# Gathering the experts' token rows as ready-made high and low parts

## The reference

```python
comb = jnp.einsum("tk,tke->te", w, jax.nn.one_hot(eid, N_EXPERTS, dtype=jnp.float32))
y = jnp.zeros((B * S, D), jnp.float32)
for e in range(N_EXPERTS):
    hid = jax.nn.silu(t @ w1[e]) * (t @ w3[e])
    y = y + comb[:, e:e + 1] * (hid @ w2[e]).astype(jnp.float32)
```

## Time and profile before

| | |
|---|---|
| median of 3 runs | 2202.26 us (2196.2 to 2210.37) |
| profiled execution, its time | 2203.71 us |
| its span in the trace | 2201.9 us |
| busy over the span | PE 96%, PEld 84%, DVE 75%, ACT 50%, POOL 21% |
| mean granted TensorE clock | 0.978 |

### The profile page before, as it was taken

The page is one execution under the profiler, slowest core; times in us unless marked ns, Lnnn a source line. Parts: engine busy times, 40 slices in busy tenths (PEclk is TensorE's granted clock), DMA queues, the critical chain, the costliest instruction groups (busy, mean ns, idle before and its releaser), DMA issues. The chain is left out here.

```text
span 2201.9 us, 34859 instructions
## 1 busy us (share of the span) xinstructions
PE 2115.3 (96%) x13433; PEld 1839.4 (84%) x13433; DVE 1655.9 (75%) x2247; ACT 1111.8 (50%) x1291; POOL 455.8 (21%) x239
## 2 busy tenths in 40 slices
PE   6999999999999999999999998999979999999996
PEld 6998999559998998999658997999957777777775
DVE  5665887548666765778538655788789999999998
ACT  4343353334433433354324343524348888888885
POOL 8600180809004500081718100000010000000000
PEclk9999999999998999999999999999989999999999
DMA  8854564436655655464336653435649999999994
GB/s 260 267 183 141 158 213 141 143 125 226 211 176 186 232 184 178 145 200 154 134 134 211 199 193 96 153 116 166 235 155 362 369 369 378 364 362 377 367 366 171
DMA packets 238996, 484.33 MB, mean 220 GB/s; under 512 B 10612, under 2 KB 178848, under 8 KB 222528
## 3 DMA queue, kind: packets, MB, share of 16 engines
q1 hardware_dynamic: 226880, 443.58, 57.5%
q0 software_dynamic: 11424, 37.44, 5.1%
q10 hardware_dynamic: 608, 2.14, 0.2%
HBM read 482.03 MB, written 1.09 MB: 219 GB/s over the span
## 5 line engine op out<-in xcount | busy, mean ns | idle before, releaser
L748 PE MATMUL misc<-xh,ring_low 128*128 128x256 f32 x1536 | 427.9, 279 | 0.0
L747 PE MATMUL misc<-xl,high_b 128*128 128x256 f32 x1408 | 394.0, 280 | 9.4 <-DVE xl L2117 6.9
L749 PE MATMUL misc<-xh,high_b 128*128 128x256 f32 x1408 | 392.0, 278 | 0.0
L748 PEld LDWEIGHTS misc<-xh,ring_low 128*128 128x128 f32 x1536 | 291.9, 190 | 3.4
L2779 DVE TENSOR_TENSOR ring_low<-ring,high_b 128x2048 fp32r<-128x2048 f32 x128 | 287.1, 2284 | 0.0
L747 PEld LDWEIGHTS misc<-xl,high_b 128*128 128x128 f32 x1408 | 267.2, 190 | 13.7 <-DVE xl L2117 7.1
L749 PEld LDWEIGHTS misc<-xh,high_b 128*128 128x128 f32 x1408 | 267.0, 190 | 0.0
L2126 DVE TENSOR_TENSOR ring_low<-ring,high_b 128x2048 fp32r<-128x2048 f32 x88 | 226.2, 2611 | 39.7 <-ACT high_b L1613 39.7
L1890 ACT ACTIVATE high_b<-ring 128x2048 fp32r<-128x2048 f32 x124 | 235.7, 1914 | 33.9 <-DMA ring<-in_w_dram 33.0
L1644 ACT ACTIVATE arena<-arena 128x256 f32<-128x256 f32 x88 | 36.8, 418 | 427.7 <-DVE arena L2160 427.7
L1310 PE MATMUL misc<-high_b,ue 128*128 128x512 f32 x512 | 204.2, 399 | 1.9 <-DVE ue L2822 1.2
(11 more groups left out here) (426 smaller groups left out, 4964.1 us busy)
## 6 DMA issues: line engine op xcount, KB each, us to landing
ring<-in_w_dram SPq DMA_DIRECT2D x128, 1024.0 KB, 7.8
ring<-in_w_in_dram SPq DMA_DIRECT2D x72, 1024.0 KB, 5.5
ring_d<-in_w_dram SPq DMA_DIRECT2D x128, 512.0 KB, 5.2
ring<-in_ffn_w_gate_dram SPq DMA_DIRECT2D x44, 1024.0 KB, 5.4
ring<-in_ffn_w_up_dram SPq DMA_DIRECT2D x44, 1024.0 KB, 7.8
ring_d<-in_ffn_w_down_dram SPq DMA_DIRECT2D x88, 512.0 KB, 7.3
arena<-in_w_ada_dram POOLq DMA_DIRECT2D x48, 512.0 KB, 4.4
ring<-in_w_out_dram SPq DMA_DIRECT2D x20, 1024.0 KB, 4.9
```

Source lines behind the costliest of these rows:

```text
L747: pe.matmul(dst, wh, ml, start=start, stop=False, **kw)
L748: pe.matmul(dst, wl, mh, start=False, stop=False, **kw)
L749: return pe.matmul(dst, wh, mh, start=False, stop=stop, **kw)
```

## The change

The token rows are split once, ahead of all pairs: ScalarE copies u2 into uh (two instructions of 128x1024, put between the high copies of the first weights), VectorE writes u2 minus uh into ul (two of 128x1024). gather no longer reads u2 in fp32; it runs two passes, one over uh and one over ul, with fp32r matmuls against sel, which is now fp32r as well. The result of a block lies in the bank as block, expert, part, slot, in the order of ue, so that a group fills a whole bank, and ScalarE copies all 512 columns to ue in one instruction. VectorE's tokens (L2822) is gone, and ScalarE's copy sets the bank free. In ScalarE's list tokens 0 and 1 and gate3 now stand ahead of the high copy of the next pair's block 0, and tokens 2 and 3 behind it. u2, sel, both and join move to other addresses; the branch experts, which does not run here, gets two waits.

```diff
--- before.py
+++ after.py
@@ -209,6 +209,9 @@
         hidh, hidl = over("hidh", [2, SEQ]), over("hidl", [2, SEQ])
         beside(A_X)
         xh, xl = over("xh", [KD, SEQ]), over("xl", [KD, SEQ])
+        beside(A_X + 2 * KD * SEQ + NT * D)
+        sel = over("sel", [NT, 2 * CAP])
+        A_JOIN = low_at[0]
         beside(ARENA)
         x = sb("x", [P, NT, D])
         x_rows = x[:, :, :]
@@ -354,12 +357,14 @@
         comb, place = route(EP), route(EP)
         logit = route(N_GROUPS + EXPERTS)
         number = route(1)
-        at[0] = A_X
-        u2 = part([NT, D])
-        sel = part([NT, 2 * CAP])
+        at[0] = A_JOIN
+        join = part([CAP])
+        assert at[0] <= A_OSQ
+        u2 = y2
+        uh, ul = (a[:, :, :].rearrange("p a b -> p (a b)").rearrange("p (t d) -> p t d", t=NT) for a in (xh, xl))
+        at[0] = A_HID + 4 * SEQ
         both = part([2, 2 * BLK])
-        join = part([CAP])
-        assert at[0] <= A_X + 2 * KD * SEQ
+        assert at[0] <= A_X
         at[0] = A_OUT
         out_e = part([D])
         selw = part([NT, 2 * CAP])
@@ -461,6 +466,9 @@
         rows_in = sem("rows_in")
         gained = sem("gained")
         zeroed = sem("zeroed")
+        u2_rows = sem("u2_rows")
+        uh_ready = sem("uh_ready")
+        ul_ready = sem("ul_ready")
         rt_in = sem("rt_in")
         rt_exp = sem("rt_exp")
         y_final = sem("y_final")
@@ -478,7 +486,6 @@
         xs_high = sem("xs_high")
         xs_low = sem("xs_low")
         xh_ready = sem("xh_ready")
-        ue_high = sem("ue_high")
         y_ready = sem("y_ready")
         scattered = sem("scattered")
         lo_ready = sem("lo_ready")
@@ -1290,14 +1297,22 @@
 
                 def gather(i, groups, before=0):
 
-                    for q in groups:
-                        b = claim3(i, TOKENS[q] - before)
-                        for kk in range(2):
-                            k = 2 * q + kk
-                            for t in range(NT):
-                                mm = pe.matmul(b[:, kk * P:(kk + 1) * P], u2[:, t, k * P:(k + 1) * P], sel[:, t, :],
-                                               start=(t == 0), stop=(t == NT - 1))
-                        mm.then_inc(filled, 1)
+                    banks = {}
+                    for part_, rows_ in enumerate((uh, ul)):
+                        if before and part_ and groups[0] == 0:
+                            pe.wait_ge(ul_ready, NT)
+                        for q in groups:
+                            if not part_:
+                                banks[q] = claim3(i, TOKENS[q] - before)
+                            b = banks[q].rearrange("p (k h s c) -> p k s h c", k=2, h=2, s=2)
+                            for kk in range(2):
+                                k = 2 * q + kk
+                                for t in range(NT):
+                                    mm = pe.matmul(b[:, kk, part_], rows_[:, t, k * P:(k + 1) * P],
+                                                   sel[:, t, :].rearrange("p (h c) -> p h c", h=2),
+                                                   start=(t == 0), stop=(t == NT - 1))
+                            if part_:
+                                mm.then_inc(filled, 1)
 
                 def gate_up_e(i, half, j):
 
@@ -1355,7 +1370,9 @@
 
                 g0 = 2 * DEPTH * NF
                 pe.wait_ge(sel_ready, 1)
-                gather(0, range(4), 16)
+                pe.wait_ge(uh_ready, NT)
+                gather(0, range(0, 2), 16)
+                gather(0, range(2, 4), 16)
                 pe.wait_ge(zero_ready, 1)
                 with pe.Fori(0, EXPERTS // 2) as i:
                     for j in TOKENS:
@@ -1924,9 +1941,8 @@
 
                     for q in groups:
                         wait_pair_filled(act, i, F_TOKENS[q] if turn_ == 0 else q - 3)
-                        act.activation(ue[:, 2 * q:2 * q + 2, :, 0:CAP],
-                                       bank_of(M0 + TOKENS[q])[:, 0:2 * P].rearrange("p (a b c) -> p a b c", a=2, b=2),
-                                       ACT.Copy).then_inc(ue_high, 1)
+                        act.activation(ue[:, 2 * q:2 * q + 2, :, :].rearrange("p a b c -> p (a b c)"),
+                                       bank_of(M0 + TOKENS[q]), ACT.Copy).then_inc(drained[(M0 + TOKENS[q]) % 4], 1)
 
                 def first_weights(i, part_):
 
@@ -1953,11 +1969,11 @@
                     for c in range(CPE):
                         high_d(i, 1, c)
                     products(i, 1, 7)
+                    tokens(i, (0, 1))
+                    gate3(i, 1)
                     if not last:
                         high(i + 1, 0, 0)
-                    tokens(i, range(2))
-                    gate3(i, 1)
-                    tokens(i, range(2, 4))
+                    tokens(i, (2, 3))
                     if not last:
                         for x in range(1, 3):
                             high(i + 1, 0, x)
@@ -2033,6 +2049,10 @@
             act.activation(stat[:, 58:60], konst[:, K_CNT:K_CNT + 2], ACT.Exp)
             wait_slot_read(act, RING["wout2"] + 3)
             for x_ in range(4):
+                if x_ == 2:
+                    for t in range(NT):
+                        act.wait_ge(u2_rows, t + 1)
+                        act.activation(uh[:, t, :], u2[:, t, :], ACT.Copy).then_inc(uh_ready, 1)
                 n = RING["moe"] + x_
                 act.wait_ge(loaded[n % SLOTS], LOAD * (n // SLOTS + 1))
                 act.activation(high_b[:, n % SLOTS, :], ring[:, n % SLOTS, :], ACT.Copy).then_inc(high_in[n % SLOTS], 1)
@@ -2738,8 +2758,8 @@
 
             def token_rows(t):
                 dve.wait_ge(gained, t + 1)
-                link(dve.scalar_tensor_tensor(out=token(t), in0=token(t), scalar=rstd[:, t:t + 1],
-                                              in1=by_part(shrow), op0=ALU.mult, op1=ALU.add))
+                dve.scalar_tensor_tensor(out=token(t), in0=token(t), scalar=rstd[:, t:t + 1],
+                                         in1=by_part(shrow), op0=ALU.mult, op1=ALU.add).then_inc(u2_rows, 1)
 
             def placing():
 
@@ -2765,13 +2785,13 @@
 
                 def choose(e):
 
-                    dve.tensor_tensor(by_half(sel), iota.unsqueeze(1).unsqueeze(1).to_broadcast([P, NT, 2, CAP]),
+                    dve.tensor_tensor(by_half(sel[:, :, :]), iota.unsqueeze(1).unsqueeze(1).to_broadcast([P, NT, 2, CAP]),
                                       both_of(place, e), ALU.is_equal).then_inc(sel_ready, 1)
 
                 def weigh(e, i):
 
                     dve.wait_ge(sel_ready, i + 1)
-                    dve.tensor_tensor(by_half(selw), by_half(sel), both_of(comb, e), ALU.mult).then_inc(selw_ready, 1)
+                    dve.tensor_tensor(by_half(selw), by_half(sel[:, :, :].bitcast(F32)), both_of(comb, e), ALU.mult).then_inc(selw_ready, 1)
 
                 def low(i, half, x):
                     wait_pair_split(dve, high_in, half, i, x)
@@ -2812,16 +2832,6 @@
                         dve.wait_ge(lo_ready, i * 4 + (2 * half + c + 1))
                         j = OUT[half] + c
                         dve.tensor_tensor(out_e[rows_, cs], bank_of(M0 + j)[rows_, :], lo_rows[rows_, cs], ALU.add)\
-                            .then_inc(drained[(M0 + j) % 4], 1)
-
-                def tokens(i, groups):
-
-                    for q in groups:
-                        dve.wait_ge(ue_high, i * 4 + (4 + q + 1))
-                        j = TOKENS[q]
-                        dve.tensor_tensor(ue[:, 2 * q:2 * q + 2, :, CAP:2 * CAP],
-                                          bank_of(M0 + j)[:, 0:2 * P].rearrange("p (a b c) -> p a b c", a=2, b=2),
-                                          ue[:, 2 * q:2 * q + 2, :, 0:CAP].bitcast(F32), ALU.subtract)\
                             .then_inc(drained[(M0 + j) % 4], 1)
 
                 def first_weights(i, outs_of=None):
@@ -2846,22 +2856,22 @@
                     outs(i, 0)
                     for c in range(CPE):
                         low_d(i, 1, c)
-                    tokens(i, range(2))
                     hidden_e(i, 1)
                     if not last:
                         low(i + 1, 0, 0)
-                    tokens(i, range(2, 4))
                     if last:
                         outs(i, 1)
                     else:
                         first_weights(i + 1, i)
 
                 choose(0)
+                for t in range(NT):
+                    dve.wait_ge(uh_ready, t + 1)
+                    dve.tensor_tensor(ul[:, t, :], u2[:, t, :], uh[:, t, :].bitcast(F32), ALU.subtract)\
+                        .then_inc(ul_ready, 1)
                 weighing()
                 weigh(0, 0)
-                tokens(-1, range(1))
                 low(0, 0, 0)
-                tokens(-1, range(1, 4))
 
                 for j in (-5, -2, -1):
                     wait_pair_drained(dve, 0, j - 4)
@@ -2906,6 +2916,8 @@
 
                 weighing()
```

(2 more changed lines are left out.)

## The result

| | before | changed |
|---|---|---|
| median | 2202.04 us (2196.2 to 2210.37, 9 runs) | 2217.11 us (2213.45 to 2228.1, 9 runs) |
| ratio of the times | | 1.0071, 95% interval 1.005 to 1.0092 |
| profiled execution, its time | 2203.71 us | 2213.63 us |
| its span | 2201.9 us | 2211.7 us |
| mean granted TensorE clock | 0.978 | 0.979 |

The account below looks back on a forecast made before the run. Two chains, VectorE's own list and ScalarE's high parts, were taken to bound a pair within 0.11 us of each other. TensorE 0, ScalarE's list +10 and the stretch ahead 0 gave +10 us: 2212 us, range 2192 to 2230.

Parts of the forecast that it names:

- the rivals: Other outcomes: VectorE's saving counts, 2185 us (0.07); narrow fp32r matmul slow, 2252 (0.15); gather halves, 2198 (0.06).
- part 5: ScalarE's list: block 0's high part behind gate3 delays all later high parts by 1.00 us a pair.
- part 4: ScalarE's token copies of 128x512 instead of 128x256: 0.8 us more a pair, paid only where ScalarE is on the chain.
- Part 1: VectorE loses four token subtractions a pair, 1.33 us of its list; alone this would leave VectorE at 32.64 us.
- What comes back: gate3 no longer delayed by late weights of block 0: 0.2 to 0.3 us a pair back, leaving +0.65 us.
- Part 2: TensorE's gather as 32 fp32r matmuls of 128 columns a pair at 0.11 us each: nothing gained or lost.
- the second rival: TensorE's gather: narrow fp32r matmul, or its result's write, slow; 0.22 us apiece, +50 us, 2252 us; chance 0.15.
- the third: Rival on TensorE's gather: it halves to 0.055 us apiece, -4 us, 2198 us; chance 0.06.
- four times slower: TensorE's split gather output: how much slower the write must be to show above the passes' 0.11 us.
- Part 3: Gather order: first group full 0.45 us later, so ScalarE waits near 0.7 us ahead of tokens 0.
- Part 6: Ahead of the pairs: added copies, subtractions and a gather of 24 matmuls at 0.19 us; sum 0, bounds -1 and +3.
- the slack of 0.11: Distance in us between VectorE's own list and ScalarE's high parts in the followed pair; taken as used up.

Follow-up runs that it names:

- experiment 2: The kernel before with only ScalarE's new order (tokens 0, 1 and gate3 ahead of the high part of block 0): 2209.34 us, ratio 1.0018.
- experiment 12: The changed kernel with 8 instead of 16 gather matmuls ahead of joined, leaving out some tokens of the second tile: 2202.95 us, ratio 0.9999.
- experiment 6: The changed kernel with half the bytes of each w2 load: 2215.44 us, ratio 1.0069 against the kernel before.
- experiment 4: The kernel before without VectorE's four token subtractions in each pair of the loop; ScalarE's copy sets the bank free: 2200.75 us, ratio 0.9988.
- experiment 1: The changed kernel with ScalarE's old order, high part of block 0 ahead of tokens 0, 1 and gate3: 2212.76 us, ratio 1.0026.
- experiment 7: The kernel of experiment 1 with half the bytes of each w2 load: 2202.85 us, ratio 1.0002 against the kernel before.
- experiment 11: The changed kernel with nothing but the gather done group by group, both parts of a group before the next: 2216.85 us, ratio 1.0059.
- experiment 9: The changed kernel with ScalarE's list as token copy 0, high of block 0, gate3, copy 1, high of block 1, tokens 2 and 3: 2200.71 us, ratio 0.9993.
- experiment 3: The changed kernel with block 0's high part first, tokens 0 and 1, gate3, and tokens 2 and 3 behind block 1: 2206.83 us, ratio 1.0006.

## Why the prediction was right

The time on record, 2212 us, is 5 us under the measured 2217.11, which lies inside the range and inside the forecast's own bounds (2206 to 2218); it fell within the 1% that had the chance of 0.77, and none of the rivals came. It was taken that only 1% can be told from no change; the interval of 0.2% either way tells 0.7% clearly. The mechanism held; two terms of the sum were off in opposite directions: the loop 10 us forecast, 8.8 measured, and the stretch ahead 0 forecast, 2.4 measured.

**The chain (part 5) is right term by term.** From gate3 to block 1: 3.12 forecast, 3.03 in the trace. The high part of block 0 starts 0.28 behind gate3. Then from block 1's high part to the end of block 3's 6.78, where the earlier trace rows gave 1877.65 - 1870.89 = 6.76; low part 2.32 (2.39 by the earlier trace rows); to the scatter 2.00 (1.99); to joined's end 20.68 (20.67). The only thing that grew is the piece from gate3 to block 1. Part 5 puts it all under the move of the high part of block 0, though its 3.12 holds two copies at the new width from part 4; experiment 2, by one pair of each kernel, splits the 0.91 into 0.49 for the order and 0.42 for the wider copies. Experiment 12 shows the part on TensorE, experiment 6 that no load is in it.

**Part 1, that VectorE's saving isn't realised,** is shown twice: by VectorE's 31.5 us of idle time in the window of 480 (7.0 in the earlier trace rows), and by experiment 4, where the saving alone gave 0.2 us a round out of 1.33.

**What comes back.** The forecast took off 0.2 to 0.3 us a round for gate3 no longer standing behind late weights: +0.65 net. Measured is +0.59 net: 34.84 in the pair that I followed against 33.93 is 0.91, and the mean of the round before (34.24) was already 0.3 above that quiet pair. The waits for w1 and w3 went from 29.7 to 2.5 us, as that argument had it, and with half the bytes of w2 the kernel before has a round of 33.97, close to that of the quiet pair. So the cause given is borne out, but the size had no row behind it: half of the 0.35 us that was read is 0.18, not 0.2 to 0.3, and that the net came out at 0.59 against 0.65 is in part luck. What the argument missed is its other half: late weights also keep the old order from its gain once VectorE's subtraction is gone (experiments 1 and 7).

**Part 2, TensorE's gather.** The 16 matmuls run from 1868.62 to 1869.46 + 1.06 = 1870.52, 1.90 us. Eight last 1.06 with the last one's own 0.28, (1.06 - 0.28) / 7 = 0.11 us from start to start: the value of both neighbours. The result is written as two runs of 64 columns with 64 between, at the same 0.11. So neither the second rival nor the third happened. The Trainium skill, "PSUM — Partial Sum Buffer", section Specifications (TRN2), has any non-contiguous access slow a matmul significantly: no slowing is seen in this trace for runs of 64 columns. But a small one could hide. 256 columns take 0.11 us as well, so by proportion 128 columns need some 0.055 (an estimate), and a write up to twice as slow would not show; the forecast's "four times slower" is a slip.

"FP8 and Floating Point Precision", section TensorE Precision Notes, of the Trainium skill has true fp32 take four passes through the array. This trace agrees with that at 512 columns. The scatter of the kernel before is two fp32 matmuls, which appear as four instructions; they start at 1882.03, and the next instruction starts 1.71 us later, at 1883.74:

```profile
1883.74 1.90 PE L1324 MATMUL misc<-arena 128*128 128x64 f32 x16
```

That is 0.86 us for one fp32 matmul, against 0.23 for an fp32r one of the same width (1881.80 to 1882.03). What failed is the step from there to the gather: an fp32r matmul of 128 columns does not cost a quarter of an fp32 one (0.22 us) but half, since its price stays at 0.11 instead of falling to 0.055. So the gather stayed at 32 instructions of 0.11 us a pair. That the load of the stationary columns sets this price, as the forecast guessed, no run tested.

**Part 3.** ScalarE waits 0.69 us for the first group, forecast 0.7; experiment 11 shows that it costs nothing, as something waits behind it anyway.

**Part 6, ahead of the pairs, is the term that was mis-sized:** 0, with bounds of -1 and +3; measured +2.4 in this trace. From the norm copy to the first once-a-pair line the four kernels with the old gather take 49.8 to 50.5 us, the ten with the new one 51.6 to 52.6: the means lie 2.0 us apart. The first expert matmul starts 32.7 to 32.8 us behind the norm copy in all ten, 31.6 to 31.7 in the four: the first 1.06 us. The scatter behind the first 32 expert matmuls starts 41.5 to 41.7 us behind it, against 39.9: 1.6 us. The rest of the 2.4 was not traced. The term said 24 matmuls at 0.19 and a copy of 0.6. TensorE's timeline of the changed kernel:

```profile
1624.65 1.97 PE L1311 MATMUL misc<-sel,xh 128*128 128x128 f32 x8 [4.35 <-DVE sel L2788]
1626.92 1.97 PE L1311 MATMUL misc<-sel,xl 128*128 128x128 f32 x8 [0.30 <-DVE xl L2870]
1628.69 1.91 PE L1311 MATMUL misc<-sel,xh 128*128 128x128 f32 x8
1630.40 1.91 PE L1311 MATMUL misc<-sel,xl 128*128 128x128 f32 x8
1633.28 0.79 PE L1325 MATMUL misc<-high_b,ue 128*128 128x512 f32 x1 [0.98 <-ACT ue L1944]
```

24 matmuls take 1626.92 to 1632.31, 5.39 us, 0.22 apiece, and the copy with its waits 0.97. The 0.19 was a mean over a stretch in which the granted clock rose from 0.50 to 1.00 (between 1631.5 and 1631.75). The windows show that, the gather and the stretch behind it (columns as in the earlier trace rows), the kernel before:

```profile
1627.00:1634.27 7.27, 6.04 (x32) 5.86 (x33) 5.91 (x14) 2.33 (x5) 0.00 (x0) 0.68 0.01 3
1634.27:1637.40 3.13, 3.13 (x13) 2.45 (x14) 3.13 (x2) 2.99 (x4) 0.00 (x0) 1.00 0.00 0
```

and the changed one:

```profile
1624.65:1633.28 8.63, 7.35 (x32) 6.98 (x33) 8.38 (x13) 5.47 (x7) 0.00 (x0) 0.50 0.01 3
1633.28:1636.43 3.15, 3.15 (x7) 2.48 (x8) 3.15 (x3) 3.15 (x4) 0.00 (x0) 0.50 0.00 0
```

Before, the granted clock was 0.68 in the gather and 1.00 behind it. Changed, with 0.30 and 0.98 us of standing still in between, it was at 0.50 throughout, the 1.2 GHz level, and stayed there for 3.15 us more: 7 expert matmuls instead of 13. That the gaps kept the clock down is argued from these rows, not tested. The forecast also leant on the last low part as cover for this stretch. It was ready sooner, 37.2 us behind the norm copy instead of 37.9, and TensorE no longer waited for it: its own matmuls filled the stretch, the first seven in 3.15 us instead of 1.6. At 0.23 us each the 32 matmuls would have ended near 40.1 us behind the norm copy, an estimate, 0.1 to 0.2 us later than before. So the late start by itself would have been nearly covered, and the low clock is what the term left out.

**Smaller slips in the working.** "No engine has 1 us of slack" is wrong for ScalarE: 33.97 - 30.07 = 3.9 us, as part 4 itself says. The new round with the slack of 0.11 taken off is 33.93 - 0.11 + 1.00 = 34.82 us, not 34.9; the pair that was followed took 34.84. Not each low part waits for its high part: that of block 2 doesn't.

**What stays open.** The rows add up to +11.9 us (8.8 + 2.4 + 0.7), the medians to 15. With the rest of the launch moving by up to 13.6 us between executions, one trace can't place the remaining 3. Of the 11.9, the 0.7 of the tail and 0.4 of the 2.4 lie within what the traces scatter by. That the move of u2, sel, both and join to other addresses is free was not tested by itself; experiment 9, which keeps it, has a shorter round than the kernel before. Nor did I settle how the 34.3 us of experiments 1 and 3 divide between late weights, wide copies and gate3.

## What to carry to other kernels

When several chains run within 1% of each other, work taken off one engine can buy almost nothing (here 1.33 us gave 0.2), and a move in another engine's list can cost more than the work saved. Follow one round from release to release, and count what stands between the release and the next piece of the closing chain. Put a long piece of work that depends on nothing in front of a release where the engine would stand waiting anyway (experiment 9), not behind it; the same instructions, differently placed, were worth 0.95 us of a round of 34.8. Here a late load ahead of gate3 was paid for by VectorE and all that follows it; that wider copies between the two made it dearer is likely from experiment 1's rows, but was not tested by itself.

## What the runs showed of the hardware

- An fp32r matmul with 128 moving columns takes 0.11 us from start to start at the full clock, like one of 256 columns and a pass of 64 plain fp32 columns, and 0.22 us at half the clock (16 starts from 1626.92 to 1630.40 are 3.48 us). An fp32r matmul of 512 columns takes 0.23 us at the full clock and 0.43 at half of it (six starts from 1633.87 to 1636.43 are 2.56 us).
- A plain fp32 matmul of 512 columns takes 0.86 us, 3.7 times as long as an fp32r one; at 128 columns it takes 0.22, twice as long.
- An output of two runs of 64 fp32 columns with 64 between costs an fp32r matmul of 128 columns nothing that can be seen: 0.11 us. A slowing of the write by less than two would not have shown.
- ScalarE's copy of 128x512 from the bank lasts 0.60 us alone and two of them 1.08, one of 128x256 0.38 and two 0.64; that of 64x512, half the partitions, is no shorter (two in 1.07).
- The granted clock of TensorE rose from 0.50 to 1.00 between 1631.5 and 1631.75 in the kernel before, while its gather ran without a gap, and between 1636.25 and 1636.5 in the changed one, seven expert matmuls behind a gather that had stood still for 0.30 us and was followed by 0.98 us of standing still.
